# Moving 24 modulation blocks on VectorE from the attention steps to the gated unit behind the S5 layer

## The reference, cut to what matters

```python
cond = jax.nn.silu(c)
for i in range(DEPTH_2):
    mod = cond @ ada_w[i] + ada_b[i]                      # 6 x 1024 numbers
    sh1, sc1, g1, sh2, sc2, g2 = jnp.split(mod[:, None, :], N_MOD, axis=-1)
    h = _modulate(_rmsnorm(x, norm_mix_g[i]), sh1, sc1)
    ...                                                   # y = S5 mixer for i = 0
    x = x + g1 * y
    h = _modulate(_rmsnorm(x, norm_mlp_g[i]), sh2, sc2)
    x = x + g2 * _sq_relu_mlp(h, mlp_w1[i], mlp_w2[i])
```

## Time and the profile before

| what | us |
|---|---|
| median of 3 runs | 2213.03 |
| the profiled execution | 2213.58 |
| its span, first to last instruction | 2211.9 |
| TensorE busy | 2134.6 |
| VectorE busy | 1215.4 |
| ScalarE busy | 702.6 |
| GpSimd busy | 148.8 |

### The profile page before, as it was taken

How to read it: one execution, slowest core, us unless ns; L and a number is a source line. 1 busy time by engine, 2 the same in 40 slices (tenths; PEclk the granted TensorE clock), 3 DMA queues, 4 the chain that set the end, 5 groups by cost and what they waited for, 6 DMA issues and landing times.

```text
span 2211.9 us, 24806 instructions
## 1 busy us (share of the span) xinstructions
PE 2134.6 (97%) x9914; PEld 1428.7 (65%) x9914; DVE 1215.4 (55%) x1726; ACT 702.6 (32%) x1059; POOL 148.8 (7%) x157
## 2 busy tenths in 40 slices
PE   7999998997999989999999999999999999999997
PEld 3454444333333335678888888878777788888886
DVE  1776863344433336895474555566986646343434
ACT  4123422110000005323242231346884424232331
POOL 0011100002310004000000000000110000000000
PEclk9999999999999999999999999999999999999999
DMA  9756465999999993211345454423342222222221
GB/s 389 288 185 215 142 241 208 401 427 427 420 426 426 428 427 127 79 68 62 133 160 186 156 177 163 143 77 116 126 156 81 96 95 77 95 95 95 95 96 57
DMA packets 112808, 434.71 MB, mean 197 GB/s; under 512 B 7982, under 2 KB 13106, under 8 KB 98760
## 3 DMA queue, kind: packets, MB, share of 16 engines
q1 hardware_dynamic: 92872, 361.46, 42.6%
q0 software_dynamic: 19840, 71.93, 9.0%
HBM read 430.57 MB, written 6.36 MB: 198 GB/s over the span
## 4 chain that ended last, share of the span: by engine, by line
PE 60%; PEld 15%; DVE 7%; DMA 7%; issue 6%; ACT 2%; DVEq 2%; POOLq 0%; SPq 0%; PEldq 0%; POOL 0%; ACTq 0%
PE PS L1132 7%; PE PS L740 6%; PE PS L743 6%; PE PS L744 6%; PE PS L840 6%; PEld PS L740 5%; PEld PS L744 5%; PEld PS L743 4%; DMA work<-in_w_dn 4%; PE PS L1155 4%; PE PS L1399 3%; PE PS L1403 3%; PE PS L1402 3%; PE PS L1169 2%; PE PS L969 2%
## 5 line engine op out<-in xcount | busy, mean ns | idle before, releaser
L744 PE MATMUL PS<-work_f32r,work_f32r 128*128 128x512 f32 x1168 | 454.4, 389 | 0.0
L2155 DVE TENSOR_TENSOR ring_f32r<-ring,work_f32r 128x2048 fp32r<-128x2048 f32 x100 | 227.8, 2287 | 140.5 <-ACT work_f32r L1553 140.1
L740 PE MATMUL PS<-work_f32r,work_f32r 128*128 128x512 f32 x768 | 299.5, 390 | 2.1 <-DVE work_f32r L2902 1.1
L743 PE MATMUL PS<-work_f32r,ring_f32r 128*128 128x512 f32 x768 | 298.8, 389 | 0.0
L1553 ACT ACTIVATE work_f32r<-ring 128x2048 fp32r<-128x2048 f32 x100 | 190.2, 1910 | 304.0 <-DMA ring<-in_mlp_w 247.0
L744 PEld LDWEIGHTS PS<-work_f32r,work_f32r 128*128 128x128 f32 x1168 | 219.3, 188 | 45.6
L1132 PE MATMUL PS<-work 128*64 128x512 f32 x752 | 170.6, 597 | 2.2 <-ACT work L1761 2.2
L740 PEld LDWEIGHTS PS<-work_f32r,work_f32r 128*128 128x128 f32 x768 | 144.2, 188 | 33.3 <-DVE work_f32r L2902 1.5
L743 PEld LDWEIGHTS PS<-work_f32r,ring_f32r 128*128 128x128 f32 x768 | 144.2, 188 | 29.8 <-issue 0.2
L740 PE MATMUL PS<-h_f32r,work_f32r 128*128 128x512 f32 x400 | 155.9, 390 | 1.4 <-DVE work_f32r L2175 1.4
L743 PE MATMUL PS<-h_f32r,ring_f32r 128*128 128x512 f32 x400 | 155.6, 389 | 0.0
(11 more groups left out here) (423 smaller groups left out, 3357.8 us busy)
## 6 DMA issues: line engine op xcount, KB each, us to landing
work<-in_w_gu SPq DMA_DIRECT2D x47, 2048.0 KB, 21.9
ring<-in_mlp_w SPq DMA_DIRECT2D x64, 1024.0 KB, 5.2
work<-in_w_dn SPq DMA_DIRECT2D x24, 2048.0 KB, 24.6
ring<-in_w_gu SPq DMA_DIRECT2D x16, 2048.0 KB, 24.2
work<-in_ada_w_2T POOLq DMA_DIRECT2D x48, 512.0 KB, 3.6
work<-in_ada_w_2T POOLq DMA_DIRECT2D x16, 1536.0 KB, 6.8
ring<-in_m_w_in SPq DMA_DIRECT2D x20, 1024.0 KB, 5.2
work<-in_w_adaT POOLq DMA_DIRECT2D x8, 2048.0 KB, 10.4
```

Source lines behind the costliest of these rows:

```text
L740: mm = nc.tensor.matmul(PS[:, bank + k, :], f32r(w_of), f32r(hi(c)), start=first and c == 0, stop=False)
L743: nc.tensor.matmul(PS[:, bank + k, :], f32r(wlo), f32r(hi(c)), start=False, stop=False)
L744: mm = nc.tensor.matmul(PS[:, bank + k, :], f32r(w_of), f32r(lo(c)), start=False, stop=last and c == 3)
L2155: tt(f32r(ring[:, s, at, :]), ring[:, s, at, :], f32r(tiles[s][:, at, :]), ALU.subtract).then_inc(w_split, 1)
```

## The change

`ADA_BLOCKS` becomes 24 and `ADA_GLU` is 12: the attention steps compute blocks 0 to 23, and blocks 24 to 47 become 12 pairs (`mod_pair`), loaded by GpSimd as 1024 KB each into two new buffers of two blocks (`ada_pair`). Chunks n = 0 to 5 of the gated unit run two pairs each before they take the gate. The sum with the bias is split, and the MLP's gain is made at n = 6.

```diff
-ADA_BLOCKS = NMOD * KC
-ADA_DONE = ADA_LATE + ADA_BLOCKS
+ADA_BLOCKS = 3 * KC
+ADA_GLU = (NMOD * KC - ADA_BLOCKS) // 2
+ADA_DONE = ADA_LATE + ADA_BLOCKS + ADA_GLU
...
+        ada_pair = [wk(24576, 2, D), wk(26624, 2, D)]
...
-            sp.wait_ge(ada_used, 2 + ADA_DONE)
+            sp.wait_ge(ada_used, 2 + ADA_LATE + ADA_BLOCKS)
...
+            pool.wait_ge(s5_mm, KC)
+            for j in range(ADA_GLU):
+                pool.wait_ge(ada_used, 2 + ADA_LATE + ADA_BLOCKS + max(j - 1, 0))
+                pool.dma_start(ada_pair[j % 2], A["ada_w_2T"][0, (ADA_BLOCKS + 2 * j) * P:(ADA_BLOCKS + 2 * j + 2) * P, :]
+                               .rearrange("(n p) k -> p n k", p=P)).then_inc(ada_loaded[j % 2], 16)
...
-                    for q in range(3):
+                    for q in range(2):
                         mod_block(q)
...
-                mod_block(3 * n)
-                mod_block(3 * n + 1)
+                mod_block((3 * n + 1) // 2)
                 attention_weights(n)
-                mod_block(3 * n + 2)
+                if n % 2 == 0:
+                    mod_block(3 * n // 2 + 1)
...
+            def mod_pair(j):
+
+                dve.wait_ge(ada_loaded[j % 2], 16 * ((ADA_LATE + ADA_BLOCKS) // 2 + j // 2 + 1))
+                for n in range(2):
+                    w, q = ada_pair[j % 2][:, n, :], ADA_BLOCKS + 2 * j + n
+                    done = stt(w, w, 1.0, cond2[:], ALU.mult, ALU.mult, accum_out=mod2[:, 0, q:q + 1])
+                done.then_inc(ada_used, 1)
...
                 for n in range(4 * i, 4 * i + 4):
+                    if n < ADA_GLU // 2:
+                        mod_pair(2 * n)
+                        mod_pair(2 * n + 1)
+                    elif n == ADA_GLU // 2:
+                        dve.drain()
+                        late = slice(ADA_BLOCKS, NMOD * KC)
+                        tt(mod2[:, 0, late], mod2[:, 0, late], col("ada_b0", ADA_BLOCKS, NMOD * KC - ADA_BLOCKS), ALU.add)
+                        dve.drain()
+                        norm_gain(4, mod2[:, 0, 4 * KC:5 * KC], "nmlp0")
                     dve.wait_ge(gate_sig, n + 1)
```

More of the change, by code:

```diff
@@ L2288, in _ @@
             head_var(HEADS - 1)
-            tt(mod2[:, 0, :], mod2[:, 0, :], col("ada_b0", 0, 48), ALU.add)
+            tt(mod2[:, 0, 0:ADA_BLOCKS], mod2[:, 0, 0:ADA_BLOCKS], col("ada_b0", 0, ADA_BLOCKS), ALU.add)
             dve.drain()
@@ L2292, in _ @@
             norm_gain(3, mod2[:, 0, KC:2 * KC], "nmix0")
-            norm_gain(4, mod2[:, 0, 4 * KC:5 * KC], "nmlp0")
             dve.drain()
```

## The result

The changed kernel takes 2233.36 us (median of 4 runs, 2230.82 to 2235.43) against 2212.72 (4 runs, 2212.02 to 2213.48): a ratio of 1.009, 95% interval 1.0074 to 1.0106. It is 0.9% slower, by 20.6 us.

A forecast was written before the change was run, and what follows sets the result against it. TensorE was taken to bound the attention steps, and VectorE to be full behind the fifth gate. -2.8 + 9.4 + 4.5 + 4.65 + 3.2 = +18.95 us on the profiled 2213.58 gave a median of 2232.0 us, range 2221 to 2239.

The forecast's parts named there:

- Attention: Attention steps: TensorE gets back only its waits on VectorE, 1.9 + 0.9 us; -2.8 us, bounds 0 and 4.9.
- The 0.9 for the exponentials: Attention steps: TensorE's 0.9 us wait for ScalarE's exponentials, taken to go back to VectorE's maxima.
- Loads set the pace: Gated unit, first half: pair loads make each chunk take 7.7 us, so TensorE gets the fourth chunk's bank late; +9.4 us.
- meetings: Gated unit: two pair loads issued near SyncE's 1024 KB refills land later; +4.5 us, bounds 0 and 4.9.
- The tail: Behind chunk 4's gate: chunk 5's blocks 4.6, sum, gain and drains 0.5, less 0.45 slack; +4.65 us.
- the slack at ScalarE's square: Gated unit's end: ScalarE's square started 0.45 us behind VectorE's last chunk, counted as all the slack there.
- The clock: TensorE at half speed after long waits, at the fourth chunk and MLP 0's start: 1.6 us each, +3.2; bounds 0 and 6.4.
- VectorE's pace alone: Rival, gated unit: 1024 KB land within about 3.6 us, a chunk takes VectorE's 6.6 us; +8.3, 2221.3 us; chance 0.08.
- Late loads with no meetings and a clock that holds: Rival, gated unit: only late loads and added tail work cost, besides attention's gain; +11.3, 2224.3 us; chance 0.25.
- Faster: Rival, attention steps: VectorE and its loads bound them, 18.9 us come back; -7.9, 2205 us; chance 0.04.

The follow-up runs named there:

- kept warm: Changed kernel with dummy TensorE matmuls filling most of its waits for banks and the wait ahead of the norm: 2231.53 us, ratio 1.0082 to the kernel before.
- tail pairs early: Changed kernel with chunk 5's two pairs run ahead of chunk 4's gate, everything computed: 2230.54 us, ratio 1.0087 to the kernel before.
- the attention half alone: Kernel before with blocks 24 to 47 left out and its gated unit unchanged: 2211.39 us, ratio 0.9992 to the kernel before.
- no loads: Changed kernel loading only the first two pairs, the other ten reusing those buffers, VectorE's instructions the same: 2223.25 us, ratio 1.0051 to the kernel before.
- Half loads: Changed kernel loading only the first block (512 KB) of each pair from pair 2 on: 2225.88 us, ratio 1.0054 to the kernel before.

## Why the prediction was right, point by point

The forecast was 2232.0 us and the median is 2233.36. The account of the spans: the start -1.3, attention -2.1, experts and S5 -0.4, A and B +16.6, C +4.9, D +1.3, the rest -0.6, together +18.4.

- **Attention, forecast -2.8: measured -2.1.** The mechanism was right, TensorE's waits on VectorE and nothing of VectorE's 27.5 us. Of the two waits in the earlier trace rows only the 1.9 us were VectorE's. The 0.9 for the exponentials is in the changed profile unchanged, so it is ScalarE's own pace, with maxima on time. The prediction read it as a wait that goes back to VectorE's maxima, and there it was wrong. The other 1.3 us by which the router's transfer is early lie ahead of the first scores and are not the change's, and the 0.4 of experts and S5 are less than two executions of one program differ by.
- **Loads set the pace, forecast +9.4, meetings +4.5: measured +14.8.** The add of chunk 3 ends at 1066.86, 37.3 us behind the start of the split; TensorE would want the bank 22.6 us behind it (1055.9 - 1033.32). The landing alone was 5.2 us against 5.1, a pair's release to issue 0.38 against 0.3. What the meetings cost stands in the adds: the chunk without a meeting took 7.9 us (forecast 7.7), the two with one 10.1 each, so 2.2 us apiece and 4.4 together, against 4.5. That loads and meetings are the cause is shown by three runs with A 8.8 and 5.0 shorter and 4.2 longer. One detail was wrong: the chain ran through pairs 3, 5 and 7, not 2, 4 and 6. VectorE did wait for pairs 2 and 4 (2.53 and 1.75 us), but the pair after each landed later still, so by these times an earlier pair 2 or 4 would only have moved the wait. And what a load met was not the refill alone: ahead of pair 3 stood also pair 2's own 1024 KB, issued 2.3 us before it.
- **The tail, forecast +4.65: measured +4.6.** C grew by 4.9, and 0.4 of it came back in D, the size of the slack at ScalarE's square: at full clock D is 6.9 us (kept warm, and tail pairs early) and was 7.3. The 0.5 estimated for the sum, the gain and the drains holds: the adds of chunks 5 and 6 are 3.2 us apart (1104.89 to 1108.09) where 2.7 stood.
- **The clock, forecast 1.6 + 1.6: measured 1.6 in B and 1.6 in D** in this profile, against the warm kernel. That the sum fits so closely is partly luck. The share in B is absent from the profile of tail pairs early, which has the same waits there. The share in D fell on the norm's own matmuls, ahead of MLP 0, and not on the start of MLP 0 as forecast. And the kernel before loses 0.4 in D in some executions: 7.68 us, with 3 to 4 us of half speed, in its second profile and with the attention half alone, 7.31 without.
- **The rivals.** VectorE's pace alone is what no loads brings out: 2223.3 with some loss by the clock, against the 2221.3 given for it without. Late loads with no meetings and a clock that holds has no run of its own. The changed profile refutes it, with landings of 6.6 to 7.8 us for pairs 2 to 5 against 5.2 for pairs 6 and 7, and with granted 0.50. Half loads, at 2225.9, is near its 2224.3, but had both meetings and half speed. Faster (the chain of the earlier trace rows read as a bound) is refuted by the attention half alone.

What stays open is why the experts take up to 3 us more in one execution than in another of the same program. The kernel before has half-speed stretches at 372, 543, 717 and 775 us, and the changed one at 368, 538 and 712, but no run here ties them to the time.

## What to carry to other kernels

Work that is moved into an engine's idle time is free only at the instructions between which that idle time lies. VectorE had over 40 us of idle time in this stage, and the change put the blocks in the one place where each microsecond is handed on: between two hand-overs of a bank. Where a load belongs to each piece of moved work, work out the period of its buffers (use, issue, landing, and what other queue's bytes are ahead) and set it against the pace of the engine that waits, before looking at how busy anything is. Judge what leaves a stage by the waits of the engine that bounds it, not by the chain that ended last, which ran through 12 us of loads for a gain of 2. And where two executions of one program differ by 3 us, compare stretches of the traces and not totals.

## What the runs showed of the hardware that I had not expected

- A transfer of 1024 KB issued by GpSimd lands in 5.2 us when it meets little else (pairs 6 and 7). Pair 3 took 7.8, with two such ahead of it: SyncE's refill issued 3.4 us before and pair 2 issued 2.3 us before. With one MB more from SyncE it took 10.8, so that MB cost 3.0. Not every MB ahead has that price. Pair 10 was issued 2.95 us behind a load of SyncE of the same size and landed in 5.3, and pair 11, issued 2.3 us behind pair 10, in 5.8:

```profile
1071.68 0.39 SPq L429 DMA_DIRECT2D ring<-in_mlp_w  x1
...
L685 POOL DMA_DIRECT2D work<-in_ada_w_2T x1: 713/713/713, 1074.6 to 1074.6; - x1
...
DMA to landing us min/median/max: 5.3/5.3/5.3
```

  What decides between the two prices no run here varies alone. The Trainium skill ("DMA: Bandwidth & Descriptors", Issuing engines are not separate DMA queues) says that transfers of all engines run on the same 16 DMA engines and interleave; that a foreign load delays a landing agrees. The fit in the Trainium skill ("DMA: Bandwidth & Descriptors", Anatomy of one DMA) gives an estimate of 4.4 us for the lone transfer, and the measured 5.2 is longer.
- Half speed of TensorE costs nothing while another engine's hand-over ends the wait behind it: of 10.2 us at granted 0.50 (1054.3 to 1064.5) none reached the end, since A is as long with a warm clock. The 3.4 us at 1067.9, where TensorE was busy throughout, cost 1.6.
- Two executions of the kernel before differ by 3 us in where the gated unit begins, more than the whole gain of the attention half.
